# Rank differences laid out rank outermost, a pick in halving sums, and a 512-column projection in the first layer's routing

## The reference

```python
q = (xb @ w_q).reshape(T, PEER_HEADS, 2, PEER_DQ // 2)          # 8 heads, 2 halves of 128
s = jnp.einsum('thpd,hpnd->thpn', q, keys)                       # 128 sub-keys per half
s_top, i_top = lax.top_k(s, PEER_TOPK)                           # 16 best of each half
cand = s_top[:, :, 0, :, None] + s_top[:, :, 1, None, :]         # 256 sums
cidx = i_top[:, :, 0, :, None] * PEER_NKEYS + i_top[:, :, 1, None, :]
best, sel = lax.top_k(cand, PEER_TOPK)                           # 16 best pairs
eidx = jnp.take_along_axis(cidx, sel, axis=-1)
g = jax.nn.softmax(best, axis=-1)
act = gelu(einsum('td,thkd->thk', xb, u[eidx]))
out = einsum('thk,thkd->td', g * act, v[eidx])
```

## Time and profile before

| | us |
|---|---|
| median of 3 runs | 3166.14 (3163.36 to 3167.25) |
| the profiled execution | 3168.7 |
| its span | 3166.9 |
| PE busy | 2542.6 (80%) |
| DVE busy | 1975.4 (62%) |
| ACT busy | 1168.2 (37%) |
| POOL busy | 1133.9 (36%) |
| mean granted PE clock | 0.887 of full |

### The profile page before, as it was taken

One profiled execution on the slowest core, in us unless ns is written; L12 is line 12 of the kernel. 1 busy time (PEld: TensorE's weight loads), 2 busy tenths in 40 slices (PEclk: granted clock), 3 DMA queues, 4 the chain that ended last, 5 costly groups with the idle time before them and its releaser, 6 DMA issues. The chain is left out here.

```text
span 3166.9 us, 41622 instructions
## 1 busy us (share of the span) xinstructions
PE 2542.6 (80%) x15562; PEld 1901.4 (60%) x15562; DVE 1975.4 (62%) x4467; ACT 1168.2 (37%) x2244; POOL 1133.9 (36%) x1013
## 2 busy tenths in 40 slices
PE   5978699899166777888789999888777797777776
PEld 3778546587166777777678777577745552222222
DVE  3566535478896899877744444466543799845544
ACT  3422235327682333333333333342234443333332
POOL 1024100331006676566565555202303354433331
PEclk8985689899598898998899999888678899999999
DMA  5210141147039999999999999631002799999996
GB/s 206 77 31 1 62 160 36 60 150 251 0 166 381 407 406 403 365 384 397 390 400 406 405 406 405 242 97 31 9 1 90 302 415 422 421 422 422 421 421 247
DMA packets 211896, 816.93 MB, mean 258 GB/s; under 512 B 22680, under 2 KB 41688, under 8 KB 178032
## 3 DMA queue, kind: packets, MB, share of 16 engines
q0 software_dynamic: 110592, 536.92, 41.9%
q1 hardware_dynamic: 101104, 277.35, 23.5%
HBM read 796.37 MB, written 17.83 MB: 257 GB/s over the span
## 5 line engine op out<-in xcount | busy, mean ns | idle before, releaser
L1978 PE MATMUL ps<-pair_ring,pair_diag 128*128 128x512 f32 x1024 | 476.3, 610 | 144.4 <-ACT pair_diag L2052 141.7
L2162 DVE CUSTOM_DVE_ANT_0 pair_ring<-pair_ring,hT 128x1024 f32<-128x1024 f32 x256 | 313.1, 1223 | 212.0 <-DMA pair_ring<-in_uv_rows,eid 203.7
L1978 PEld LDWEIGHTS ps<-pair_ring,pair_diag 128*128 128x128 f32 x1024 | 187.2, 192 | 423.4 <-ACT pair_diag L2052 227.5
L1942 POOL DMA_INDIRECT pair_ring<-in_uv_rows,eid x256 | 267.4, 1045 | 391.7 <-PE ps L1978 366.8
L2310 POOL DMA_INDIRECT sparse_ring<-in_v_rows,eidT x256 | 286.0, 1117 | 294.9 <-PE ps L2359 223.0
L2310 POOL DMA_INDIRECT sparse_ring<-in_u_rows,eid x256 | 349.2, 1364 | 113.9 <-issue 67.5
L119 PE MATMUL ps<-h_hi,peer_uh 128*128 128x256 f32 x1024 | 310.6, 303 | 83.7 <-DVE peer_ul L2422 76.0
L2448 DVE CUSTOM_DVE_ANT_0 sparse_ring<-sparse_ring,hT 128x1024 f32<-128x1024 f32 x256 | 303.8, 1222 | 40.4 <-DMA sparse_ring<-in_u_rows,eid 32.9
L120 PE MATMUL ps<-h_lo,peer_uh 128*128 128x256 f32 x1024 | 300.0, 293 | 1.1 <-issue 1.1
L121 PE MATMUL ps<-h_hi,peer_ul 128*128 128x256 f32 x1024 | 299.3, 292 | 0.0
L119 PEld LDWEIGHTS ps<-h_hi,peer_uh 128*128 128x128 f32 x1024 | 206.8, 202 | 147.3 <-DVE peer_ul L2422 94.9
(11 more groups left out here) (413 smaller groups left out, 5437.6 us busy)
## 6 DMA issues: line engine op xcount, KB each, us to landing
peer_u<-in_uT SPq DMA_DIRECT2D x128, 512.0 KB
peer_v<-in_v_rows SPq DMA_DIRECT2D x128, 512.0 KB
ada_slab<-in_ada_w SPq DMA_DIRECT2D x20, 2048.0 KB, 9.1
proj_slab<-in_w_fm SPq DMA_DIRECT2D x38, 512.0 KB
route_slab<-in_w_pq SPq DMA_DIRECT2D x32, 512.0 KB, 6.9
peer_gates<-dense_stage SPq DMA_DIRECT2D x4, 4096.0 KB, 13.1
peer_gates<-peer_gates SPq DMA_DIRECT2D x32, 512.0 KB
out_slab<-in_w_out SPq DMA_DIRECT2D x16, 512.0 KB, 3.7
```

Of the source, the lines that this page charges most:

```text
L1942: nc.gpsimd.indirect_dma_start(out=ring[:, s % R], out_offset=None, in_=d["uv_rows"], in_offset=bass.IndirectOffsetOnAxis(ap=eid[:, s:s + ...
L1978: mm = nc.tensor.matmul(ps[:, 4 + 2 * t + half, :], diag[:, s % DG, :], ring[:, s % R, D_MODEL + half * BANK:D_MODEL + (half + 1) * BANK], ...
L2162: nc.vector.tensor_tensor_reduce(out=row, in0=row, in1=hT[:, s // NS], scale=1.0, scalar=0.0, op0=ALU.mult, op1=ALU.add, accum_out=dots[:, ...
```

## The change

Four edits in the first layer.

1. `dist` and `by_slot` are laid out with the rank a outermost: `[P, 2, TOPK, nt * HK]`. A difference now writes 256 adjacent values, and `by_slots` reads the sub-key numbers at a step of 16 and writes them adjacent.
2. `pick` becomes a tensor_scalar (equal to 0), a tensor_tensor (times the number), and sums that halve the 16 ranks: tensor_tensor over 2048, 1024 and 512 elements in bf16 and a last one over 256 into the fp32 result. Each waits for the one before.
3. The high and low inputs of both token groups lie in one tile `h2_both` `[P, 2, 2, DC, CTX]`, and the projection takes both groups in one matmul of 512 columns, 24 in all for each column.
4. `phase_mixed` has no tiles of its own for `peer_uh` and `peer_ul`; it uses the context half of `h2_both`, which nothing reads any more.

```diff
-                dist0 = sb(st, f"route_dist{l}", [P, 2, nt * HK, TOPK], BF16)
-                dist1 = slab[:]....rearrange("p (j k a) -> p j k a", j=2, a=TOPK)
+                dist0 = sb(st, f"route_dist{l}", [P, 2, TOPK, nt * HK], BF16)
+                dist1 = slab[:]....rearrange("p (j a k) -> p j a k", j=2, a=TOPK)
...
-                spare = sb(st, f"route_spare{l}", [P, nt * HK, TOPK], BF16)
+                spare = sb(st, f"route_spare{l}", [P, TOPK, nt * HK], BF16)
...
-                            for a, b, hi, low in hp:
-                                for k in range(DC):
-                                    mm = product(nc, ps[:, c % 2, a - lo:b - lo], (wh[:, c % 2, k, :], wl[:, c % 2, k, :]),
-                                                 (hi[:, k, :], low[:, k, :]), k == 0, k == DC - 1)
+                            for k in range(DC):
+                                mm = product(nc, ps[:, c % 2, :].rearrange("p (a t) -> p a t", a=2), (wh[:, c % 2, k, :], wl[:, c % 2, k, :]),
+                                             (hp[:, 0, :, k, :], hp[:, 1, :, k, :]), k == 0, k == DC - 1)
...
-                                last = nc.scalar.activation(dist[g][:, j, :, a], ranks[:, 1 + 2 * j],
+                                last = nc.scalar.activation(dist[g][:, j, a], ranks[:, 1 + 2 * j],
...
-                            f = idx[:, g, j].rearrange("p t h a -> p (t h) a")
-                            nc.scalar.activation(by_slot[j].rearrange("p (th k) a -> p th k a", k=TOPK), bc(f, 2, TOPK),
+                            f = idx[:, g, j].rearrange("p t h a -> p a (t h)")
+                            nc.scalar.activation(by_slot[j].rearrange("p a (th k) -> p a th k", k=TOPK), bc(f, 3, TOPK),
...
-                            d = dist[g][:, j].rearrange("p k a -> p (k a)")
-                            nc.vector.scalar_tensor_tensor(out=d, in0=d, scalar=0.0, in1=by_slot[j].rearrange("p k a -> p (k a)"),
-                                                           op0=ALU.is_equal, op1=ALU.mult).then_inc(chosen, 1)
+                            d = dist[g][:, j].rearrange("p a k -> p (a k)")
+                            step(nc.vector.tensor_scalar(d, d, 0.0, None, ALU.is_equal))
+                            nc.vector.tensor_tensor(d, d, by_slot[j].rearrange("p a k -> p (a k)"), ALU.mult).then_inc(chosen, 1)
                             dve.wait_ge(chosen, 2 * g + j + 1)
-                            return nc.vector.tensor_reduce(found[:, j, :, HK * g:HK * (g + 1)],
-                                                           dist[g][:, j].rearrange("p (t k) a -> p t k a", t=nt), AX, ALU.add)
+                            w = TOPK // 2 * nt * HK
+                            while w > nt * HK:
+                                step(nc.vector.tensor_tensor(d[:, 0:w], d[:, 0:w], d[:, w:2 * w], ALU.add))
+                                w //= 2
+                            one, other = (d[:, x * w:(x + 1) * w].rearrange("p (t k) -> p t k", t=nt) for x in range(2))
+                            return nc.vector.tensor_tensor(found[:, j, :, HK * g:HK * (g + 1)], one, other, ALU.add)
...
-                uh = sb(st, f"peer_uh{l}", [P, 2, DC, P], F32R)
-                ul = sb(st, f"peer_ul{l}", [P, 2, DC, P], F32R)
+                uh, ul = (x.rearrange("p k t -> p (k t)").rearrange("p (r k c) -> p r k c", r=2, k=DC) for x in lent)
...
+                    both = sb(st, f"h2_both{l}", [P, 2, 2, DC, CTX], F32R)
...
-                            hp = [(0, CTX, *(sb(st2, f"h2c_{x}{l}", [P, DC, CTX], F32R) for x in ("hi", "lo"))), (CTX, T, *own)]
+                            hp = [(CTX * i, CTX * (i + 1), both[:, 0, i], both[:, 1, i]) for i in range(2)]
...
-                            phase_route(l, lo, hp, q, (l + 1, 0, 12), nt, eid, eidT, gate, iT, jT, gT)
+                            phase_route(l, lo, both, q, (l + 1, 0, 12), nt, eid, eidT, gate, iT, jT, gT)
...
-                    phase_mixed(l, own, hT, eid, eidT, gate)
+                    phase_mixed(l, [both[:, i, 1] for i in range(2)], [both[:, i, 0] for i in range(2)], hT, eid, eidT, gate)
```

More of the change, by code:

```diff
@@ L1536, in phase_route @@
                 ranks = sb(st, f"route_ranks{l}", [P, 4, nt * HK])
-                dist0 = sb(st, f"route_dist{l}", [P, 2, nt * HK, TOPK], BF16)
-                dist1 = slab[:].rearrange("p a b c -> p (a b c)").bitcast(BF16).rearrange("p (j k a) -> p j k a", j=2, a=TOPK)
+                dist0 = sb(st, f"route_dist{l}", [P, 2, TOPK, nt * HK], BF16)
+                dist1 = slab[:].rearrange("p a b c -> p (a b c)").bitcast(BF16).rearrange("p (j a k) -> p j a k", j=2, a=TOPK)
                 dist = (dist0[:], dist1)
@@ L1541, in phase_route @@
                 places = found[:].rearrange("p a t k -> p (a t k)").bitcast(U32)[:, 0:4 * nt * HK].rearrange("p (a n) -> p a n", a=4)
-                spare = sb(st, f"route_spare{l}", [P, nt * HK, TOPK], BF16)
-                by_slot = (spare[:], kT[:].rearrange("p c k -> p (c k)").bitcast(BF16).rearrange("p (k a) -> p k a", a=TOPK))
+                spare = sb(st, f"route_spare{l}", [P, TOPK, nt * HK], BF16)
+                by_slot = (spare[:], kT[:].rearrange("p c k -> p (c k)").bitcast(BF16).rearrange("p (a k) -> p a k", a=TOPK))
                 bmax = sb(st, f"route_bmax{l}", [P, nt, PH])
@@ L2189, in _, with phase_mixed @@
                         add_back(1)
-        def phase_mixed(l, hp, hT, eid, eidT, gate):
+        def phase_mixed(l, hp, lent, hT, eid, eidT, gate):
             nt = CTX // P
@@ L2490, in build @@
                 nt = 2
-                own = [sb(st, f"h2_{x}{l}", [P, DC, T - CTX], F32R) for x in ("hi", "lo")]
+                if last_layer:
+                    own = [sb(st, f"h2_{x}{l}", [P, DC, T - CTX], F32R) for x in ("hi", "lo")]
+                else:
+                    both = sb(st, f"h2_both{l}", [P, 2, 2, DC, CTX], F32R)
                 hT = sb(st, f"hT{l}", [P, nt, D_MODEL])
```

## The result

| | before | after |
|---|---|---|
| median of runs, us | 3166.49 (3163.36 to 3167.25, n = 4) | 3131.86 (3125.72 to 3134.34, n = 4) |
| ratio | | 0.9889, 95% interval 0.9877 to 0.9902 |
| the profiled execution; its span | 3168.7; 3166.9 | 3130.53; 3128.8 |
| route: first matmul; loop's end; length of the loop | 640.41; 796.29; 155.88 | 639.90; 784.03; 144.13 |
| tail (first pick's start to last pick's end) | 50.99 | 27.59 |

The kernel became 34.6 us faster; 3131.6 was forecast.

What follows compares the result with a forecast made beforehand. Late ScalarE score copies were taken to set the loop's end, ScalarE and VectorE taking turns the tail. Loop 11.9 plus tail 22.6 gave 34.5 us, 3168.7 to 3134.2, median 3131.6; range 3124 to 3147, own range 3127 to 3138.

Steps and rivals of the forecast that it cites:

- Rival B: ScalarE's spread becomes slow through its stepped reads, 17.2 us; no change overall, 3166 us; chance 0.04.
- operand traffic: VectorE pick: two-byte adjacent operands halve the traffic, so half the fp32 slopes, 6.5 us a pick.
- of other operations: VectorE pick: the slow bf16 rows, 4.42 us for 4096, do not apply to tensor_scalar and tensor_tensor.
- Rival A: VectorE does not speed up on two-byte operands; picks of 11.5 or 13.7 us, time 3151 or 3160; chance 0.09.
- rival C: TensorE projection: the two-run operand halves the matmul's rate, 10.9 us a column, time 3210 us; chance 0.03.
- D: Shared tile's placement slows or speeds the mixed stage by 1%, 12 us: 3120 or 3143; chance 0.06, both ends.
- The loop: Loop over 16 query columns: column 13's scores come 7.6 us earlier from ScalarE, 4.3 more from the projection; gain 11.9.
- VectorE's ready time: Loop: VectorE free for column 11 at 743.1, ready for column 13 at 758.0, 1.4 us before its scores.
- The tail: From the first pick's start: four picks of 6.5 us, 1.86 and a wait end at 28.4 instead of 50.99; gain 22.6.
- a forecast wait for the last pick: Tail: ScalarE ends at 21.9 us, VectorE is ready at 21.4, so it waits 0.5 us.

Runs made afterwards that it cites:

- the joint operation: Changed kernel with compare and product in one scalar_tensor_tensor over 4096 bf16 on the new layout, halving sums kept: 3134.55 us, ratio 0.9903.
- routing edits alone: Kernel before with only the new layout and new pick; projection still 48 matmuls of 256 columns, tiles separate: 3135.10 us, ratio 0.9903.
- the moved pick: Changed kernel with the first pick moved into VectorE's wait before column 13, its spread to column 12: 3130.36 us, ratio 0.9890.

## Why the prediction came out right

The mechanism held: the routing became 35.1 us shorter where 34.5 was forecast, 11.75 in the loop (11.9) and 23.40 in the tail (22.6). That the median came within 0.3 us of the forecast is luck: single runs of the changed kernel lie between 3125.72 and 3134.34.

**Edit 1.** Taken 0.44 us a difference, measured 0.40; spreads 3.51 to 3.60 where 3.8 was taken. Rival B (the spread slow through its stepped reads) is out: a read that moves by 64 bytes after every 16 values, with adjacent writes, cost nothing. The Trainium skill (SBUF — State Buffer, Door 1: The DMA port swizzle) was weighed for this. By the line rule, fewer than two hits in a 16-byte line cost time. The rise from 8 to 16 bytes in the bf16 row (0.575 to 1.14 us) fits it. That 8 bytes, two hits a line, already cost 0.575 against 0.40, and that the fp32 row rises only from 0.45 to 0.51, don't fit, and there the measurement decides. What inside the chip makes only the two-byte write slow, no run here shows.

**Edit 2.** Taken 6.5 us a pick, measured 6.49, with tensor_scalar at 1.22, the product at 2.29 and the halvings at 2.41 for three. The times that followed from operand traffic held, and so did the exclusion of the slow bf16 rows as "of other operations": the joint operation kept its 4.42 us on the same data. Operand traffic as the cause isn't shown, and the joint operation speaks against it as a general reason, for its operands are the same two-byte ones and it gained nothing. Rival A is out. An estimate by the Trainium skill (VectorE: DVE Perf Modes, The perf-mode tier table), with four elements a cycle for a bf16 tensor_scalar and two for a tensor_tensor, gave the same 6.5, and 1.22 and 2.29 us agree with it.

**Edit 3.** Matmul starts are (757.17 - 755.36)/8 = 0.226 us apart, the rate of the 512-column rows, so an operand in two runs costs nothing extra, and rival C is out. A column takes 9.28 us where it took 9.57, and column 13's sub-scores came 4.17 us earlier, 4.3 predicted. How much reaches the end depends on what else is late: 2.9 us with ScalarE in the way, 3.9 without.

**Edit 4.** Predicted 0. The stretch behind the start of the dense gates took 2312.2 and 2311.7 us in the two kernels with separate tiles (before, routing edits alone), and 2305.8 to 2316.0 in the nine profiles with the shared one. In the mixed stage itself, the matmuls that read `peer_vh` take 1042.5 and 1043.7 us from the first start to the last with separate tiles, and 1038.3 to 1046.8 with the shared one. The placement makes no difference that can be seen, and the 2.45 us of the span that lie behind the routing are within what that stretch varies by. D is out at its 12 us.

**The loop.** Predicted 11.9, measured 11.75. One detail was wrong: a wait of 3.14 us stands before column 13, and none over 2 was forecast. The step that failed is VectorE's ready time ("It was free at 749.61 - 6.48 = 743.1"): I moved TensorE's columns earlier by the projection's gain and held VectorE where it was. It was free for column 11 at 741.19 - 1.15 = 740.04, which counted from the first projection is 2.6 us sooner than before. Of these, 1.2 come from columns 0 to 3, where VectorE waits for TensorE's columns (column 4 starts 46.77 us behind the first projection, 47.98 before), 0.9 from a shorter meeting with GpSimd, and 0.5 from the wait before column 10 that is gone. The gain was not touched, because scores and not VectorE set column 13's start in both accounts. The candidate sum met GpSimd again (1.08 us against 0.42 alone and 1.97 before), but at 696 us, ahead of columns at which VectorE waits anyway: nothing was lost.

**The tail.** Predicted 28.4, measured 27.59; 0.3 of the difference is VectorE's own work (27.9 forecast). The other 0.5 was a forecast wait for the last pick. In each of two rounds ScalarE took 16 x 0.04 us less for the differences and 0.3 less for the spread, and that took the wait away: ScalarE ended the last spread at 804.52 + 3.61 = 808.13, VectorE came to it at 809.25. With 1.1 us between them the two engines are nearly level in the tail, which is why the moved pick found ScalarE next.

## What to carry to other kernels

When two engines take turns in a stretch, price a change to either one against the other left as it is: here the layout alone gave the tail 3.3 us, the pick alone 1.7, both 23.4. And when a layout is changed for one engine, price what the other engine then reads: the reduce lost 2.6 us each time. Write two-byte results of ScalarE to adjacent places, and sum in halves with tensor_tensor; the scalar_tensor_tensor and the tensor_reduce of this kernel took 4.42 us for 4096 two-byte values, the 1.04 ns an element of its fp32 rows. Before an engine's idle time is filled, ask whose chain is next late, and whether what it waits for can be made to come earlier: that made the loop 3.4 us shorter, where filling made the routing 2.2 us longer.

## What the runs showed of the hardware that was not expected

- ScalarE writing bf16 at a step of 16 bytes or more takes 1.07 to 1.14 us for 256 elements, and fp32 at the same steps 0.51. So at these steps a strided two-byte write is slower than a four-byte one.
- VectorE's tensor_reduce over 16 bf16 values at a step of 512 bytes takes 7.08 us for 4096, 4.42 where they are adjacent.
- A VectorE tensor_scalar over 256 values took 1.24 us beside a GpSimd subtract, 0.29 alone.
- bf16 tensor_tensor in short runs of 8, 4 and 2 elements keeps nearly all of its speed: 2.62 us for the three halvings, against 2.41 in one run.
